# The last down product with the weights as the moving operand, and squares, norm and output with the tokens on the partitions

## The reference, cut to what matters

```python
def rmsnorm(x, g):
    xf = x.astype(jnp.float32)
    y = xf * lax.rsqrt(jnp.mean(xf * xf, axis=-1, keepdims=True) + EPS)
    return (y * g.astype(jnp.float32)).astype(x.dtype)

def swiglu(h, w_gate, w_up, w_down):
    return (jax.nn.silu(h @ w_gate) * (h @ w_up)) @ w_down
...
        h = rmsnorm(x, ln_gains[i, 2])
        x = x + 0.5 * swiglu(h, ffn_w_gate[i, 1], ffn_w_up[i, 1], ffn_w_down[i, 1])
    return rmsnorm(x, final_gain)
```

## Time and profile before

| what | before |
|---|---|
| median of 3 runs (lowest to highest) | 897.39 us (897.33 to 897.64) |
| the profiled execution | 896.31 us |
| its span in the trace | 894.3 us |
| TensorE, matmul busy | 880.2 us, 98% |
| TensorE, weight load busy | 778.8 us, 87% |
| VectorE / ScalarE busy | 631.0 us, 71% / 471.8 us, 53% |
| mean transfer rate | 178 GB/s |

### The profile page before, as it was taken

One profiled execution on the slowest core, in us unless ns is written; L12 is line 12 of the kernel. 1 busy time (PEld: TensorE's weight loads), 2 busy tenths in 40 slices (PEclk: granted clock), 3 DMA queues, 4 the chain that ended last, 5 costly groups with the idle time before them and its releaser, 6 DMA issues.

```text
span 894.3 us, 12774 instructions
## 1 busy us (share of the span) xinstructions
PE 880.2 (98%) x5416; PEld 778.8 (87%) x5416; DVE 631.0 (71%) x719; ACT 471.8 (53%) x564; POOL 34.2 (4%) x49
## 2 busy tenths in 40 slices
PE   7999999999999999999999999999999999999996
PEld 6888888889998988888888888888889888888896
DVE  5997776668777698777666797776564898776541
ACT  5765554445555565555454465555454675555441
POOL 1580000000000000000000000000000000000000
PEclk9999999999999999999999999999999999999998
DMA  7786655565444447555566475655564276555611
GB/s 248 225 248 199 195 177 180 177 205 172 142 141 143 141 130 247 188 189 177 177 204 196 141 236 188 189 188 165 191 209 142 88 242 198 189 195 166 207 37 48
DMA packets 153849, 159.20 MB, mean 178 GB/s; under 512 B 2688, under 2 KB 152256, under 8 KB 153792
## 3 DMA queue, kind: packets, MB, share of 16 engines
q1 hardware_dynamic: 152352, 156.78, 54.6%
q10 hardware_dynamic: 1440, 1.60, 0.5%
HBM read 157.32 MB, written 1.05 MB: 177 GB/s over the span
## 4 chain that ended last, share of the span: by engine, by line
PE 97%; DVE 1%; ACT 1%; issue 0%; DVEq 0%; POOL 0%; POOLq 0%
PE psum L371 95%; PE psum L630 1%; PE psum L616 1%; PE psum L523 0%; DVE w_lo L1052 0%; DVE x L1058 0%; PE psum L516 0%; DVE soft L910 0%; ACT xg L717 0%; PE psum L414 0%; DVE w_lo L1044 0%; ACT L726 0%; DVE band L1162 0%; DVE h_all L1133 0%; DVEq L70 0%
## 5 line engine op out<-in xcount | busy, mean ns | idle before, releaser
L371 PE MATMUL psum<-xg,w_hi 128*128 128x512 f32 (+1 forms) x1664 | 491.4, 380 | 3.2 <-DVE w_lo L1044 3.2
L891 DVE TENSOR_TENSOR w_lo<-raw,w_hi 128x2048 fp32r<-128x2048 f32 (+1 forms) x150 | 336.4, 2244 | 117.6 <-ACT w_hi L708 117.6
L371 PEld LDWEIGHTS psum<-xg,w_lo 128*128 128x128 f32 x1536 | 289.6, 189 | 62.7
L708 ACT ACTIVATE w_hi<-raw 128x2048 fp32r<-128x2048 f32 (+1 forms) x150 | 279.8, 1866 | 91.0 <-PE psum L371 91.0
L371 PE MATMUL psum<-xg,w_lo 128*128 128x256 f32 x1536 | 313.3, 279 | 0.0
L371 PEld LDWEIGHTS psum<-xg,w_hi 128*128 128x128 f32 x1664 | 254.8, 189 | 6.0 <-issue 5.1
L371 PE MATMUL psum<-h_all,w_hi 128*128 128x512 f32 (+1 forms) x876 | 246.9, 368 | 0.7 <-DVE h_all L1133 0.7
L371 PEld LDWEIGHTS psum<-h_all,w_lo 128*128 128x128 f32 x768 | 144.7, 188 | 29.3
L371 PE MATMUL psum<-h_all,w_lo 128*128 128x256 f32 x768 | 160.2, 278 | 0.0
L371 PEld LDWEIGHTS psum<-h_all,w_hi 128*128 128x128 f32 x876 | 134.0, 189 | 1.5 <-issue 1.5
L743 ACT ACTIVATE scratch<-psum 128x512 f32<-128x512 f32 x44 | 26.2, 595 | 86.1 <-PE psum L371 86.1
(11 more groups left out here) (99 smaller groups left out, 409.5 us busy)
## 6 DMA issues: line engine op xcount, KB each, us to landing
raw<-in_ffn_w_up_dram SPq DMA_DIRECT2D x43, 1024.0 KB, 5.3
raw<-in_ffn_w_gate_dram SPq DMA_DIRECT2D x42, 1024.0 KB, 5.3
raw<-in_ffn_w_down_dram SPq DMA_DIRECT2D x32, 1024.0 KB, 5.0
raw<-in_ffn_w_down_dram SPq DMA_DIRECT2D x16, 768.0 KB, 4.2
raw<-in_attn_w_qkv_dram SPq DMA_DIRECT2D x12, 1024.0 KB, 5.1
raw<-in_attn_w_o_dram SPq DMA_DIRECT2D x4, 1024.0 KB, 5.0
band<-in_x_dram SPq DMA_DIRECT2D x4, 256.0 KB, 5.2
raw<-in_ffn_w_gate_dram ACTq DMA_DIRECT2D x4, 256.0 KB, 7.1
```

The source lines that it names most:

```text
L371: return nc.tensor.matmul(out, stationary, moving, start=start, stop=stop, skip_group_check=True)
L708: nc.scalar.activation(w_hi[:, n % SPL, 0:size], raw[:, n % RAW, 0:size], ACT.Copy).then_inc(hi_split, 1)
L891: nc.vector.tensor_tensor(w_lo[:, n % SPL, 0:size], raw[:, n % RAW, 0:size], w_hi[:, n % SPL, 0:size].bitcast(f32), ALU.subtract).then_inc ...
```

## The change

It touches the last FFN (f = 3) from its down product on.

- **The roles are swapped.** `token_down(o, parts, t)` holds `h_all` of 128 tokens (`t` = 0, 1) stationary and moves 512 columns of weights (`o` = 0, 1, the halves of the 1024 features): three matmuls of 512 columns for each of 22 `k`, 2 `o` and 2 `t`. The sums stand with tokens on partitions, one bank for each (t, o).
- **The weight tiles** of this product are cut anew: 4 chunks `k` by 512 columns (2 chunks in the sixth of a half), each loaded by two transfers of 256 columns, 6 tiles for each `o`, 12 in all as before. In the buffers the two 256-column pieces of one `k` lie apart, so the moving operand is read in two pieces.
- **The order.** The last two tiles of o = 1 are taken for t = 0 first and then for t = 1, so that the tokens of t = 0 are finished 18 matmuls early.
- **The residual** is turned to tokens on partitions by 16 transposes of `x` after the second tile of o = 0, into banks 0 to 3; ScalarE copies them to `x_tok`. The transposes of the result and the sums of squares on TensorE go.
- **The factor 0.5** is put into the up part of h (`half_rstd` in the place of `rstd`, the same instruction).
- **The end**, for each t: VectorE adds the product's 128x512 sums to `x_tok`, and multiplies by a row of gains (`gain_row`, loaded to all partitions by one transfer of 512 KB) and by sqrt(1024); ScalarE squares with a running sum (`accum_out`); then mean, reciprocal, root and refinement on one column, the scaling, and two transfers of 256 KB. Both halves (o = 0) of squares and gains are done earlier. The root's table is loaded ahead of the down product.

```diff
-                                if f == 3 and pair == DB - 1:
-                                    for k, c in zip(ks, (c0, c0 + 1)):
-                                        last = passes(main_part(b, 1), hi[:, c, cols], lo[:, c, cols],
-                                                      h_all[:, k, 0, :], h_all[:, k, 1, :], k == 0, k == FC - 1)
...
+                def token_down(o, parts, t):
+                    for part in parts:
+                        n = token_tile(o, part)
+                        chunks = TOKEN_CHUNKS[part]
+                        weights(n)
+                        hi, lo = [token_cols(ring[:, n % SPL, :], n, chunks) for ring in (w_hi, w_lo)]
+                        toks = slice(t * P, (t + 1) * P)
+                        for c in range(chunks):
+                            k = TK * part + c
...
+                            out = token_acc(t, o).rearrange("p (s f) -> p s f", s=2)
+                            mm(out, h_all[:, k, 0, toks], hi[:, c], start=(k == 0))
+                            mm(out, h_all[:, k, 0, toks], lo[:, c])
+                            last = mm(out, h_all[:, k, 1, toks], hi[:, c], stop=(k == FC - 1))
...
+                if f == 3:
+                    for part in range(len(TOKEN_CHUNKS)):
+                        for t in range(TT):
+                            token_down(0, [part], t)
+                        if part == 1:
...
+                            residual_transposes()
+                    for part in range(len(TOKEN_CHUNKS) - 2):
+                        for t in range(TT):
+                            token_down(1, [part], t)
+
+                    for t in range(TT):
+                        token_down(1, range(len(TOKEN_CHUNKS) - 2, len(TOKEN_CHUNKS)), t)
+                    return
...
-            out_transposes(DC - 2)
-            token_squares(6, DB - 1)
-            out_transposes(DC - 1)
...
+            def token_down():
+
+                nc.scalar.activation(row_sum[:, 0, 1:2], row_sum[:, 0, 0:1], ACT.Sqrt)
...
+                for o in range(2):
+                    for t in range(TT):
+                        act.wait_ge(x_tok_done, TT * o + t + 1)
...
+                        nc.scalar.activation(sq_junk, x_tok[:, t, o * OW:(o + 1) * OW], ACT.Square,
+                                             accum_out=token_sums[:, t, o:o + 1]).then_inc(token_squared, 1)
+                        if o == 1:
+                            root(6 + t, rstd_p[:, t:t + 1])
+                            act.wait_ge(rstd_done, 7 + t)
+                            act.wait_ge(out_gained, t + 1)
+                            nc.scalar.activation(out_tok[:, t, 0, :], out_tok[:, t, 0, :], ACT.Copy,
+                                                 scale=rstd_p[:, t:t + 1]).then_inc(out_scaled_act, 1)
+                            act.wait_ge(out_scaled_act, t + 1)
+                            act.dma_start(out_v[:, t, 0:OW], out_tok[:, t, 0, :]).then_inc(out_written, 16)
...
+                for t in range(TT):
+                    add_token_sums(1, t)
+                    token_rstd(t)
+                    nc.vector.tensor_scalar(out_tok[:, t, 1, :], out_tok[:, t, 1, :], rstd_p[:, t:t + 1], None,
+                                            ALU.mult).then_inc(out_scaled_dve, 1)
```

More of the change, by code:

```diff
@@ L36, in build_trunk @@
     DOWN_CHUNKS = [min(DC, FC - c) for c in range(0, FC, DC)]
-    assert F % GW == 0 and SEQ == 2 * P and GM * D == ROWS and D % (2 * P) == 0
+    OW = 512
+    TK = ROWS // OW
+    TOKEN_CHUNKS = [min(TK, FC - c) for c in range(0, FC, TK)]
+    assert F % GW == 0 and SEQ == 2 * P and GM * D == ROWS and D == 2 * OW
     GU_TILES = 2 * GROUPS
     DOWN_TILES = DB * len(DOWN_CHUNKS)
+    assert DOWN_TILES == 2 * len(TOKEN_CHUNKS)
     FFN_TILES = GU_TILES + DOWN_TILES
@@ L226, in tile_size, with loads @@
                 if 0 <= at < DOWN_TILES:
+                    if f == 3:
+                        return TOKEN_CHUNKS[at % len(TOKEN_CHUNKS)] * OW
                     return DOWN_CHUNKS[at % len(DOWN_CHUNKS)] * GW
             return ROWS
-        GAIN_COL = [0, DC, 2 * DC, 3 * DC, 4 * DC, 5 * DC, 7 * DC]
+        def loads(n):
+            return n // RAW + 1 + len([i for i in range(token_tile(0, 0), n + 1) if i % RAW == n % RAW])
+        GAIN_COL = [0, DC, 2 * DC, 3 * DC, 4 * DC, 5 * DC]
         POOL_SCALE_COL = 6 * DC
@@ L408, in statistics, with residual_transposes @@
                 last.then_inc(stats_done, 1)
-            def out_transposes(d):
-                pe.wait_ge(xn_done, max(d + 1, 5))
+            def residual_transposes():
                 for t in range(TT):
[L414 to L417, removed]
+                    for d in range(DC):
+                        last = nc.tensor.transpose(psum[:, 2 * t + d // 4, (d % 4) * P:(d % 4 + 1) * P],
+                                                   x[:, d, t * P:(t + 1) * P], ident[:, :])
+                    last.then_inc(x_tok_T, 1)
             def ffn(f):
@@ L703, in split_hi @@
                     return
-                act.wait_ge(raw_loaded[n % RAW], 16 * (n // RAW + 1))
+                act.wait_ge(raw_loaded[n % RAW], 16 * loads(n))
                 if n >= SPL:
@@ L761, in down @@
                     for d in (2 * pair, 2 * pair + 1):
[L762 to L765, removed]
-                            nc.scalar.activation(sq[:, d, :], x[:, d, :], ACT.Square).then_inc(sq_done, 1)
+                        y_copy(f, d)
                         if pair == DB - 1:
-                            finish_chunk(f, d)
+                            round_chunk(NEXT_NORM[f], d)
@@ L871, in _ @@
             gate_up(3)
-            down(3)
-            root(6, rstd_p)
-            act.wait_ge(out_T, 1)
-            act.wait_ge(rstd_done, 7)
-            for t in range(TT):
-                nc.scalar.activation(x_tok[:, t, 0:D // 2], bank(4 + 2 * t), ACT.Copy,
-                                     scale=rstd_p[:, t:t + 1]).then_inc(out_scaled_act, 1)
             out_v = out[0].rearrange("(t p) d -> p t d", p=P)
-            for t in range(TT):
-                act.wait_ge(out_scaled_act, t + 1)
-                act.dma_start(out_v[:, t, 0:D // 2], x_tok[:, t, 0:D // 2]).then_inc(out_written, 16)
+            token_down()
         @block.vector
@@ L971, in add_y @@
                 main = psum[:, down_bank(f, d), 0:SEQ]
-                if f == 3 and d >= DC - 2:
-                    wait_y(dve, f, d)
-                    nc.vector.scalar_tensor_tensor(out=x[:, d, :], in0=main, scalar=0.5, in1=x[:, d, :],
-                                                   op0=ALU.mult, op1=ALU.add).then_inc(x_done, 1)
-                    return
                 dve.wait_ge(y_corr, done)
@@ L998, in down @@
                         add_y(f, d)
-                        if pair == DB - 1 and f < 3:
+                        if pair == DB - 1:
                             rest_chunk(norm, d)
```

149 lines of the change are left out of this document (99 added, 50 removed).

## The result

The changed kernel takes 889.66 us (median of 4 runs, 889.62 to 890.95) against 897.36 us in the same runs of before; the ratio of the two is 0.9921 (95% interval 0.9910 to 0.9933).

A forecast was written before the change was run, and what follows sets the result against it. TensorE was taken to bound the kernel, with 97% of the span, so only its stream and the tail count. Product 2.8 us plus tail 2.1 us gave 4.9 us off 897.39, so 892.5 us, range 890.5 to 895.0 us.

The forecast's parts named there:

- the sign: Whole kernel: faster by over 0.2% at 90%, within 0.2% at 5%, slower at 5%.
- The residual's block: Last down product: 16 transposes come in, at 0.105 us each, costing 1.7 us.
- t = 0 had 0.90 us to spare: End: t = 0's 3.5 us chain fits beside t = 1's last 18 matmuls, 4.2 us, margin 0.7 us.
- The pair of operands and the two pieces: Last down product: which operand moves makes no visible difference; two pieces counting like two matmuls would give 0.240 us.
- Slower: Rival, last down product: loads of h_all no longer hide behind moving weights; product 26 us more, 919 us; 5%.
- the tail that keeps its length: Rival, end: t = 0 overruns its margin or transfers meet, 1.5 us of 2.1 lost, 894.0 us; 8%.
- 0.240: Rival, last down product: moving weights taken at 0.240 us a matmul, as two pieces of 256; 894.6 us; 8%.
- 0.213 us a matmul: Rival, last down product: an unmixed row of 512-wide matmuls runs at the clock; 887.5 us; 8%.
- the term of the product: Last down product: 0.232 us a matmul, 62.7 us with transposes in place of 65.6; VectorE begins 2.8 us earlier.
- The term of the tail: After the last matmul: only t = 1 is left, 6.6 us against 8.7, 2.1 us less.
- The reference: Starting time: the gain is subtracted from the runs' median 897.39 us, the profiled execution being 896.31 us.

The follow-up runs named there:

- four_widths: Changed kernel with one-piece weights, last down product's four parts cut into widths 512, 256, 384 with 128, and 128: 0.227 us at 512, 0.120 at 256, 0.11 at 128.
- before_early_table: Kernel before, with only the square root's table loaded ahead of the last down product: median 896.17 us, ratio to before 0.9989.
- late_table: Changed kernel without its early table load, which then falls at the root of t = 0: runs 889.85 to 891.82 us, ratio to before 0.9934.
- long_groups: Changed kernel with rows of eight 512-wide then eight 256-wide matmuls in the FFNs, in place of two and two: 893.49 us, and 893.78 us run again.

## Why the prediction was right or wrong

**Right**: the sign, the order of the steps, and that TensorE waits for nothing in the product, nor the tail of t = 1 for that of t = 0. The residual's block cost 1.76 us (forecast 1.7). t = 0 had 0.90 us to spare (0.7). The pair of operands and the two pieces made no difference. "Slower" and the tail that keeps its length did not come, nor did 0.240 or 0.213 us a matmul.

**Wrong, the term of the product**: "By columns, 0.697 us / 1536 x 512 gives 0.232 us for a 512-wide one". It is 0.227 us, which makes 263 distances 59.6 us and not 61.0: 1.4 us of the 1.7. The cause was in the prediction's own numbers. Both kinds of stretches in the earlier trace rows run at 2.4 GHz, but I gave the 0.120 us of the 256-wide ones to the load, on the sign of a weight load that is busy all the time, and divided the rest by columns. Taken as two equations, 1536 columns and 4 matmuls in 0.697 us, and 1536 columns and 6 matmuls in 0.720 us, they give 0.0115 us for a matmul and 0.424 us for 1000 columns, so 0.2285 us for a 512-wide one; with it the sum would have been 0.9 us lower. (The blocks of two and two, which cost 0.003 us more than long rows would, keep even this from 0.227.) The busy share of the load misled: its instructions are drawn with 0.19 us, more than the 0.11 us in which four_widths has one of them for each matmul.

So the product's gain is a matter of counts: the same 135,168 columns in 264 matmuls in the place of 396. Without what the blocks in it cost beyond a matmul's own 0.12 us (4.02 - 0.24 = 3.78 us before, 1.76 us after) it took 61.83 us and takes 59.63 us: 2.2 us less, of which 132 x 0.0134 = 1.8 us are the fewer matmuls, and 66 x 0.003 = 0.2 us that blocks of two and two took 0.697 and not 0.694 us. Another 0.1 us is no gain: behind the last start 512 columns are still to come, where it was 256. The last 0.1 us is left over. The blocks of other work gave 3.78 - 1.76 = 2.0 us.

**The term of the tail**: 6.6 us forecast, 6.3 us measured, so 2.4 us less than before in the place of 2.1. VectorE's scaling of 512 columns takes 0.49 us where I took ScalarE's 0.68 for both, so that the first transfer leaves earlier, and root and refinement, on one column each, take 0.81 us (883.31 to 884.12) where I took 0.93. Of the gain, 0.63 us is that no table load stands behind the last matmul (before_early_table). Loading it early isn't needed for that: left at the root of t = 0 it cost nothing (late_table). The rest needs the early finish of t = 0, without which 1.9 us go again.

**The reference**: I subtracted from 897.39 us, and named the difference of 1.1 us to the profiled execution without asking what it was. Subtracted from 896.31 us, 4.9 us give 891.4 us; the measured lower group is 889.7. The range would have been 889.4 to 893.9 us, with the result just inside, though by luck: the product's price would still have been wrong.

## What to carry to other kernels

Before you price a matmul of another width, fit a fixed part and a part for each column to two stretches of different mix: here 0.0134 us and 1 / 2.4 GHz, so the same columns in fewer, wider matmuls are worth 13 ns for each one saved, down to the 0.11 us of a 128-wide one. Which operand moves is free to choose where both fill 128 x 512, and the choice can remove a layout change at the end and let half of the output finish early: a tail behind the last matmul shrinks when it is cut into parts and the chain of the first part fits beside the product's end (3.2 us in 4.1 us here). Subtract a gain that was summed in a trace from that execution's own time.

## What the runs showed that I had not expected

- **Time is lost to stretches at 1.2 GHz that differ between executions of one program.** Beside the late rise at the start (1.1 us) there is one in the pool mixer. In four_widths and in the changed kernel, and in long_groups (columns: stretch, its length, busy time and count of TensorE, loads, VectorE, ScalarE, GpSimd, granted clock, DMA share, GB/s):

```profile
687.00:690.50 3.50, 3.50 (x21) 3.50 (x21) 0.81 (x5) 1.77 (x4) 0.00 (x0) 0.62 0.01 3
690.50:694.00 3.50, 3.50 (x19) 3.50 (x18) 0.00 (x0) 1.99 (x6) 0.00 (x0) 0.50 0.00 0
```

```profile
687.00:690.50 3.50, 3.50 (x24) 3.50 (x24) 0.81 (x5) 2.12 (x4) 0.00 (x0) 0.68 0.01 3
690.50:694.00 3.50, 3.50 (x27) 3.50 (x27) 0.00 (x1) 2.52 (x7) 0.00 (x0) 0.83 0.00 0
```

```profile
687.00:690.50 3.50, 3.50 (x33) 3.50 (x33) 1.04 (x5) 2.49 (x4) 0.00 (x0) 1.00 0.23 79
690.50:694.00 3.50, 3.50 (x33) 3.50 (x32) 0.67 (x4) 3.03 (x8) 0.00 (x0) 1.00 0.01 2
```

  The granted clock is low for twice as long in the first as in the second, and not at all in the third; the first is 1.5 us behind the second from there on, and long_groups makes up 1.5 us there.
- **A narrow matmul behind a wide one is cheap, and a wide one behind narrow ones dear**: in long_groups up to 0.236 us for the first wide ones and 0.113 us for the first narrow one, against 0.227 and 0.120 us in a steady row. Mixed rows can't be priced matmul by matmul.
